# Value weights of the second attention: projected with tokens stationary instead of transposed afterwards

## What is computed

```python
kv = (rms_norm(x_kv, kv_norm_g) @ w_ukv).reshape(B, S, MLA_HEADS, QK_NOPE_DIM + V_HEAD_DIM)
k_nope, v = kv[..., :QK_NOPE_DIM], kv[..., QK_NOPE_DIM:]      # 128 and 128 per head
...
s = (einsum('bqhd,bkhd->bhqk', qn, k_nope) + einsum('bqhr,bkr->bhqk', qr, k_rope)) * scale
p = softmax(where(mask, s, neg))
o = einsum('bhqk,bkhd->bqhd', p, v)
```

## Time and profile before

| | us |
|---|---|
| median of 3 runs | 2361.2 (2360.68 to 2364.7) |
| span of the profiled execution | 2359.5 |
| TensorE busy in it | 2296.7 (97%) |
| VectorE busy | 1599.4 (68%) |
| GpSimd busy | 1118.3 (47%) |
| ScalarE busy | 791.9 (34%) |

### The profile page before, as it was taken

How to read it: one execution, slowest core, us unless ns; L and a number is a source line. 1 busy time by engine, 2 the same in 40 slices (tenths; PEclk the granted TensorE clock), 3 DMA queues, 4 the chain that set the end, 5 groups by cost and what they waited for, 6 DMA issues and landing times.

```text
span 2359.5 us, 29934 instructions
## 1 busy us (share of the span) xinstructions
PE 2296.7 (97%) x11150; PEld 1904.4 (81%) x11150; DVE 1599.4 (68%) x1953; ACT 791.9 (34%) x1056; POOL 1118.3 (47%) x886
## 2 busy tenths in 40 slices
PE   7999998999999999999999999899999999999998
PEld 5578887888888899887878888788888887778876
DVE  7899999965586354445586666877777602558886
ACT  4311242022333155412353333444433103344423
POOL 4136652333233246433478888898895332310130
PEclk9999999999999999999999999999999999999999
DMA  4122124432332422444244444744431311141231
GB/s 153 36 81 72 53 98 126 132 134 100 115 108 95 120 64 63 130 156 152 107 143 155 149 149 159 273 175 152 163 125 50 142 44 41 63 136 41 70 107 72
DMA packets 93266, 265.73 MB, mean 113 GB/s; under 512 B 8720, under 2 KB 26392, under 8 KB 87896
## 3 DMA queue, kind: packets, MB, share of 16 engines
q1 hardware_dynamic: 75216, 194.87, 24.2%
q10 hardware_dynamic: 17928, 69.23, 8.3%
HBM read 183.57 MB, written 81.80 MB: 112 GB/s over the span
## 4 chain that ended last, share of the span: by engine, by line
PE 68%; DVE 17%; issue 9%; POOL 3%; ACT 1%; DMA 1%; ACTq 0%; POOLq 0%; SPq 0%; DVEq 0%
PE pair L1399 24%; PE pair L1066 23%; DVE pen L2327 6%; DVE top L2325 6%; PE pair L1548 4%; PE pair L1307 2%; PE pair L1237 2%; PE pair L1517 2%; POOL w_lo L919 1%; PE pair L1502 1%; PE pair L1084 1%; PE pair L1285 1%; POOL w_hi L917 1%; PE pair L1274 1%; PE pair L1160 1%
## 5 line engine op out<-in xcount | busy, mean ns | idle before, releaser
L1066 PE MATMUL pair<-actA,w_hi 128*128 128x512 f32 x2016 | 625.0, 391 | 10.1 <-ACT stage L1665 8.0
L1066 PEld LDWEIGHTS pair<-actA,w_hi 128*128 128x128 f32 x2016 | 377.0, 188 | 89.5 <-ACT stage L1665 8.4
L915 POOL TENSOR_TENSOR pad<-pad 128x1 f32<-128x1 f32 x126 | 34.2, 272 | 803.4 <-PE pair L1066 703.8
L1066 PE MATMUL pair<-actA,w_lo 128*128 128x512 f32 x1008 | 392.9, 390 | 0.0
L1399 PE MATMUL pair<-tring,wsp 128*128 128x512 f32 x1344 | 308.1, 391 | 6.3 <-DVE tring L2652 5.7
L1399 PEld LDWEIGHTS pair<-tring,wsp 128*128 128x128 f32 x1344 | 253.6, 189 | 60.6 <-issue 7.1
L919 POOL TENSOR_TENSOR w_lo<-raw,w_hi 128x1024 fp32r<-128x1024 f32 (+2 forms) x126 | 275.0, 2182 | 10.1
L1066 PEld LDWEIGHTS pair<-actA,w_lo 128*128 128x128 f32 x1008 | 189.5, 188 | 39.8
L1399 PE MATMUL pair<-tsp,wsp 128*128 128x512 f32 x768 | 184.1, 391 | 4.0 <-DVE tsp L2579 1.9
L2620 DVE TENSOR_TENSOR xB<-pair,xB 128x1024 f32<-128x1024 f32 x112 | 136.4, 1220 | 71.8 <-PE pair L1399 71.4
L1066 PE MATMUL pair<-actB,w_hi 128*128 128x512 f32 x576 | 178.2, 390 | 0.0
(11 more groups left out here) (394 smaller groups left out, 4385.5 us busy)
## 6 DMA issues: line engine op xcount, KB each, us to landing
raw<-w_in SPq DMA_DIRECT2D x80, 512.0 KB, 3.2
wraw<-w_pair SPq DMA_DIRECT2D x32, 1024.0 KB, 7.1
staged<-hid_d SPq DMA_DIRECT2D x56, 512.0 KB, 3.4
proj<-stage ACTq DMA_DIRECT2D x40, 512.0 KB, 2.7
hid_d<-hsum SPq DMA_DIRECT2D x16, 1024.0 KB, 5.0
gates<-proj ACTq DMA_DIRECT2D x24, 512.0 KB, 5.5
raw<-w_out SPq DMA_DIRECT2D x16, 512.0 KB, 3.3
hid_d<-hid SPq DMA_DIRECT2D x16, 512.0 KB, 2.8
```

Of the source, the lines that this page charges most:

```text
L1066: last = nc.tensor.matmul(pair[par][:, cols], w[:, par, wk], x[:, cols], start=(k == 0 and i == 0), stop=(k == kt - 1 and i == 2))
```

## The change

The eight units of w_ukv change roles. Units 0 to 3 are now the keys, made as before. The values are made by four units in which 128 tokens of x_kv are the stationary operand and the 512 value columns stream past, so the result has tokens on the partitions, as V2h and V2l want it. Unit u makes the token groups 2u and 2u+1; it has 2 groups x 2 contraction tiles x 3 = 12 matmuls of 128 x 512. The copy to `v4` and the transposes are gone.

All four value units need all value weights, so they lie in a part of `w_hi` and `w_lo` of their own (columns 512 to 1023 of both slots), and each value unit waits until GpSimd has split all four pieces. The pieces still come one by one through the two slots of `raw`, in the order in which SyncE issued them before, each of 128 KB. GpSimd's splits of these pieces no longer wait for TensorE's previous units, only for their load, and have no operation on `pad`.

The diff, cut to its core:

```diff
@@ misc_plan
-    uses += [("v2T", h) for h in range(MLA_HEADS)]
@@ gpsimd
-            split_units(FIRST["ukv"], N_UKV, 2)
+            split_units(FIRST["ukv"], MLA_HEADS, 2)
+            for u in range(4):
+                n, cols = FIRST["ukv"] + MLA_HEADS + u, slice(HALF + u % 2 * 256, HALF + u % 2 * 256 + 256)
+                pool.wait_ge(w_in[n % 2], (n // 2 + 1) * 16)
+                pool.wait_ge(unit_mm, FIRST["uq"])
+                nc.gpsimd.tensor_copy(w_hi[:, u // 2, cols], raw[:, n % 2, 0:256]).then_inc(w_hi_ok, 1)
+                pool.wait_ge(w_hi_ok, n + 1)
+                nc.gpsimd.tensor_tensor(w_lo[:, u // 2, cols], raw[:, n % 2, 0:256],
+                                        w_hi[:, u // 2, cols].bitcast(F32), ALU.subtract).then_inc(w_split, 1)
@@ gpsimd, first pieces of w_out_2
-                    pool.wait_ge(unit_mm, n - 1)
+                    pool.wait_ge(unit_mm, FIRST["out2"])
@@ tensor
-            for u in range(N_UKV):
+            for u in range(MLA_HEADS):
                 n = FIRST["ukv"] + u
                 product(n, n % 2, n // 2, 2, lambda k: xkv_hi[:, k, :], lambda k: xkv_lo[:, k, :])
-                if u >= 4:
-                    unit_read(pe, n - 4)
-                    transposes(("v2T", u - 4), lambda c: v4[:, u - 4, c * P:(c + 1) * P], NB)
+
+            def value_unit(u):
+                n = FIRST["ukv"] + MLA_HEADS + u
+                pe.wait_ge(w_split, FIRST["ukv"] + N_UKV)
+                pe.wait_ge(unit_out[n % 2], n // 2)
+                for half in range(2):
+                    rows = slice((2 * u + half) * P, (2 * u + half + 1) * P)
+                    for k in range(2):
+                        for i, (x, w) in enumerate(((xkv_hi, w_hi), (xkv_hi, w_lo), (xkv_lo, w_hi))):
+                            mm = nc.tensor.matmul(pair[n % 2][:, half * HALF:(half + 1) * HALF], x[:, k, rows],
+                                                  w[:, k, HALF:2 * HALF], start=(k == 0 and i == 0),
+                                                  stop=(k == 1 and i == 2))
+                mm.then_inc(unit_mm, 1)
+
+            for u in range(4):
+                value_unit(u)
@@ tensor, logits2 and values2
-                    unit_read(pe, FIRST["ukv"] + 4 + h)
+                    unit_read(pe, FIRST["ukv"] + h)
...
-                    if g < MLA_HEADS:
-                        wait_done(pe, ("v2T", h))
@@ scalar
-            for h in range(4):
-                read_unit(n, n % 2, n // 2, v4[:, h, :], ACT.Copy)
-                n += 1
-            act.wait_ge(qr_parked, 4 * 16)
             for h in range(MLA_HEADS):
-                key = ("v2T", h)
                 act.wait_ge(unit_mm, n + 1)
                 nc.scalar.copy(k2[:, 0, h, :], pair[n % 2][:, :]).then_inc(kv_hi, 1)
                 n += 1
-                wait_ready(act, key)
-                nc.scalar.copy(V2h[:, :, h * P:(h + 1) * P], by_key(mpair(key)[:, :])).then_inc(kv_hi, 1)
+            act.wait_ge(qr_parked, 4 * 16)
+            for u in range(4):
+                act.wait_ge(unit_mm, n + 1)
+                nc.scalar.copy(V2h[:, 2 * u:2 * u + 2, :].rearrange("p a b -> p (a b)"), pair[n % 2][:, :]) \
+                  .then_inc(kv_hi, 1)
+                n += 1
@@ vector
             for h in range(4):
-                n = FIRST["ukv"] + 4 + h
-                low2(n, kv_hi, 2 * h + 1, k2[:, 1, h, :], k2[:, 0, h, :]).then_inc(unit_out[n % 2], 1)
-                key, hc = ("v2T", h), slice(h * P, (h + 1) * P)
-                dve.wait_ge(kv_hi, 2 * h + 2)
-                V.tensor_tensor(V2l[:, :, hc], by_key(mpair(key)[:, :]), V2h[:, :, hc].bitcast(F32), ALU.subtract) \
-                 .then_inc(F(key), 1)
+                n = FIRST["ukv"] + h
+                low2(n, kv_hi, h + 1, k2[:, 1, h, :], k2[:, 0, h, :]).then_inc(unit_out[n % 2], 1)
+            for u in range(4):
+                n, keys = FIRST["ukv"] + MLA_HEADS + u, slice(2 * u, 2 * u + 2)
+                low2(n, kv_hi, MLA_HEADS + u + 1, V2l[:, keys, :].rearrange("p a b -> p (a b)"),
+                     V2h[:, keys, :].rearrange("p a b -> p (a b)")).then_inc(unit_out[n % 2], 1)
@@ host
+    v_cols = ukv[:, :, P:].reshape(2, P, 2, 256).transpose(0, 2, 1, 3).reshape(4, P, 256)
+    w_ukv = np.concatenate([by_unit(ukv[:, :, :P].reshape(256, -1)), v_cols], 0)
```

More of the change, by code:

```diff
@@ L407, in build @@
         rstd_kv = at("rstd_kv", 80, [P, S])
-        v4 = at("v4", 56, [P, 4, S])
         V2h = at("V2h", 168, [P, NB, HALF], F32R)
@@ L3079 @@
     ukv = a["w_ukv_2"].reshape(256, MLA_HEADS, 2 * P)
-    ukv = np.concatenate([ukv[:, :, P:].reshape(256, -1), ukv[:, :, :P].reshape(256, -1)], 1)
+    v_cols = ukv[:, :, P:].reshape(2, P, 2, 256).transpose(0, 2, 1, 3).reshape(4, P, 256)
+    w_ukv = np.concatenate([by_unit(ukv[:, :, :P].reshape(256, -1)), v_cols], 0)
     pos = a["positions_2"][0]
@@ L3089 @@
         "rel_bias": a["rel_bias"], "w_in": by_unit(w_in), "w_up": w_up, "w_out": by_unit(a["w_out"][0])[OUT_ORDER],
-        "w_pair": w_pair.reshape(STEPS, P, 4 * HALF), "w_in2": by_unit(w_in2), "w_uq": by_unit(uq), "w_ukv": by_unit(ukv),
+        "w_pair": w_pair.reshape(STEPS, P, 4 * HALF), "w_in2": by_unit(w_in2), "w_uq": by_unit(uq), "w_ukv": w_ukv,
         "w_out2": by_unit(a["w_out_2"]), "pool_w": a["pool_w_2"].transpose(1, 0, 2),
```

## The result

The changed kernel takes 2366.4 us against 2361.6 us for the kernel before, timed beside it (medians of 11 runs each). The ratio is 1.0020, with a 95% interval of 1.0013 to 1.0028: 4.8 us slower, where 4.9 us was forecast. The span of the profiled execution is 2364.5 us, against 2359.5.

The account below looks back on a forecast made before the run. TensorE, busy for 97% of the span, was taken as the bound. The wait for value pieces (2.5 us) and the lost clock (2.4) gave +4.9 on 2361.2: 2366.1 us, range 2361.3 to 2369.8.

Parts of the forecast that it names:

- The releaser: In the w_ukv stage, the old sixth unit's split at 2085.43 was released by its load landing at 2085.31, not TensorE.
- The chain of pieces: Before the value units, the last piece reuses the second's (piece 1's) slot; TensorE resumes at 2090.0 after 7.5 us idle.
- What the removal was worth: In the value units, thirty-two transposes go, at 0.79 us for eight: 3.2 us in all.
- The rate of the value matmuls: In the value units, 48 matmuls keep 0.23 us from start to start with the operands' roles exchanged.
- The clock: After the new idle time TensorE runs at half clock on the value units, losing 2.4 us, range 0 to 3.5.
- The second mask: In VectorE's queue, the second mask starts at 2105.73 against 2103.30: +2.4 us, before the clock loss.
- That the lag stays to the end: From 2110 us on TensorE bounds the attention, 39.85 of 40 us busy, so lag at the second mask stays.
- The span: The whole profiled execution: 2359.5 + 4.9 = 2364.4 us.
- Rival 1: Value pieces land in time and the kernel is faster: -5.1 us, 2356.1, if split by 2082.5; chance 6%.
- rival 3: The last value piece's load is slow too, 3.6 us or more, half clock longer: +7.7 us, 2368.9; chance 14%.
- The inner range of the forecast: Whole kernel: 2364.3 to 2368.0 us, as the clock loss goes from 1.6 to 3.5 us with small psum waits.

Follow-up runs that it names:

- before_again: The kernel before, unedited, run once more for its profile: 2361.6 us, ratio 1.0.
- parked_late: The changed kernel with the two DMAs parking the rotated queries' low half moved behind the last value piece in SyncE's queue: 2363.0 us, ratio 1.0006.
- after_again: The changed kernel, unedited, run once more on another chip: 2366.2 us, ratio 1.0020.
- v_early_turned: The changed kernel with value weights loaded and split early, plus eight unread transposes behind each of the four value units: 2360.0 us, ratio 0.9994.
- v_early: The changed kernel with the value weights loaded and split early, while TensorE still makes the query units: 2357.8 us, ratio 0.9982.
- kept_busy: The changed kernel with 32 unread matmuls added between the fourth key unit and the wait for the value pieces: 2364.0 us, ratio 1.0012.

## Why the prediction was right

The forecast was 2366.1 us and the chance of slower 49%; measured were 2366.4 us and 4.8 us slower. Point by point:

- **The releaser.** The step on which all rests, that the split of the second piece had waited for its load although the profile put it down to TensorE, holds. before_again's profile names the load for that very split. Once no wait on TensorE stands there, the split still starts 6.5 us after the issue, and in parked_late it moves with the load.
- **The chain of pieces.** Predicted were 5.7 us for piece 1, 1.9 for piece 3 and 7.5 us of idle time; measured 6.50, 2.02 and 8.07 (7.67 in after_again). The order of events is as written. The idle time is longer mostly because the key units ended sooner (the last key matmul starts 11.44 us after the stage's start, 12.01 in before), which costs nothing: the first value matmul starts 19.89 us after the stage's start (20.06 in after_again), where 19.75 was forecast (2090.0 - 2070.25).
- **What the removal was worth.** 3.2 us of transposes by the row; v_early_turned says 3.5. It was mis-sized by the slower matmul behind each group, and it didn't enter the sum.
- **The rate of the value matmuls.** 0.23 us was taken from the other role; v_early shows 10.91 us for 48.
- **The clock.** 2.4 us was the middle of three rows; measured were 13.06 - 10.91 = 2.15 us (1.83 in after_again), and kept_busy shows by a cause, not by analogy, that the idle time makes it.
- **The second mask.** +2.4 us and the clock's 2.4 make +4.8; the stage's part of the lag is 4.5 to 4.7 us. Small errors cancel in it: the wait for the pieces ended 0.14 us later than forecast and the distance from the first logits to the second mask was 0.07 longer (4.80 against 4.73), while the 48 matmuls with the lost clock took 0.34 less (13.06 against 13.4).
- **That the lag stays to the end.** Nine of the ten profiles need 255.0 to 255.1 us from the second mask to the end, whatever the stage did.
- **The span.** 2364.4 was forecast and 2364.5 measured, but that agreement is partly luck: +1.4 us ahead of the stage and -1.1 behind it don't belong to the change: before_again has 1.0 of the first and the whole of the second. The medians, which average over such accidents, carry the verdict.
- **Rival 1** didn't come true, for the reason given, but its price was right: with the pieces early the stage is 5.1 us shorter. By the medians the gain is 3.8 us (2357.8 against 2361.7), 2 to 6 by the interval.

What I mis-judged is what a quiet load costs at this place (2.0 us in parked_late; 3.6 was taken for rival 3 and 3.5 in parked_late's expectation). The inner range of the forecast, 2364.3 to 2368.0, doesn't follow from its terms either: 2361.2 + 2.5 + 1.6 is 2365.3, and with 3.5 instead of 1.6 it is 2367.2. The measured 2366.4 lies within both.

## What to carry to other kernels

When a change makes several consumers need the last piece of a stream that was used one piece at a time, its price is the arrival of the last piece less the work that used to cover it; write out the chain of slots and loads before counting what was saved. The clock comes on top of such a wait, here 1.6 to 2.2 us for 3.9 to 8.1 us of idle time. The cure was to load where a slot has unused room, and the exchange of roles then made the stage 5.1 us shorter and the kernel 3.8 us faster by the medians.

## What the runs showed of the hardware

A scaling of VectorE from SBUF to SBUF (0.75 us) doesn't run beside a GpSimd operation that started just before it or with it. It ends 0.54 to 0.56 us after that operation does: in before at 2233.12, after a subtraction that ended at 2232.56; in before_again at 2232.92, after a cast that ended at 2232.38. The starts can be as good as equal: in parked_late the scaling is shown from 2233.42 and the cast from 2233.43, and the scaling takes 1.60 us. It holds the other way round too: in the changed kernel a scaling started first, at 2231.83 and for 0.76 us, and the cast from 2231.99 took 1.49 us instead of 1.04. The Trainium skill, page "SBUF — State Buffer", section "SBUF: two separate sides", describes the port pair that these two engines share as "an exclusive lock, not a bandwidth split"; the traces agree. A stretch of up to 0.88 us (1.63 us in v_early) cost TensorE nothing in nine profiles. The one of 2.0 us cost 1.1 us, and before shows TensorE idle behind it:

```profile
2234.39 1.06 PE L1502 MATMUL pair<-cst,L 128*128 128x128 f32 x8 [0.95 <-DVE PTl L2861]
```

No run kept the two engines apart on purpose, so the 1.1 us is read from the one profile and not shown by an edit.
